# Gated linear attention inside a macaron decoder layer: the decay factors formed by running products on VectorE in place of TensorE sums, and small products grouped into fewer visits

## The reference

```python
h = h + 0.5 * swiglu(rmsnorm(h, ffn1_norm), ffn1_w_gu, ffn1_w_down)      # 1024 -> 2 x 2816 -> 1024
h = h + hybrid_mixer(rmsnorm(h, mix_norm), w_in, w_gk_up, b_gk, gla_out_norm, w_out, rel_bias)
h = h + 0.5 * swiglu(rmsnorm(h, ffn2_norm), ffn2_w_gu, ffn2_w_down)
h = h + sigmoid(rmsnorm(h, ple_norm) @ w_ple_gate) * (p @ w_ple_proj)
return rmsnorm(h, final_norm)

def hybrid_mixer(xn, ...):
    q_g, k_g, v_g, g_g, gk_lr, q_m, k_m, v_m = split(xn @ w_in)
    log_a = log_sigmoid(gk_lr @ w_gk_up + b_gk) / 16
    o_g = gla_chunked(q_g / 8, k_g, v_g, log_a)      # 4 heads, dk 64, dv 128:
                                                    # S_t = diag(exp(log_a_t)) S_{t-1} + k_t^T v_t ; o_t = q_t S_t
    o_g = rmsnorm(o_g, gla_out_norm) * silu(g_g)
    o_m = moba_attention(q_m, k_m, v_m, rel_bias)    # 8 heads of 64; at 256 tokens: causal softmax attention
    return concat(o_g, o_m) @ w_out                  # with a relative-position bias
```

## Time and profile before

| | us |
|---|---|
| median of 3 runs | 529.13 (528.93 to 530.37) |
| the profiled execution, its own time | 529.96 |
| its span | 528.0 |
| TensorE busy | 516.1 (98%) |
| VectorE busy | 329.3 (62%) |
| ScalarE busy | 274.7 (52%) |
| mean granted clock of TensorE | 0.995 |

### The profile page before, as it was taken

The page is one execution under the profiler, slowest core; times in us unless marked ns, Lnnn a source line. Parts: engine busy times, 40 slices in busy tenths (PEclk is TensorE's granted clock), DMA queues, the critical chain, the costliest instruction groups (busy, mean ns, idle before and its releaser), DMA issues.

```text
span 528.0 us, 7035 instructions
## 1 busy us (share of the span) xinstructions
PE 516.1 (98%) x2543; PEld 419.6 (79%) x2543; DVE 329.3 (62%) x436; ACT 274.7 (52%) x336; POOL 91.5 (17%) x169
## 2 busy tenths in 40 slices
PE   7999999999999999998999999999999999999994
PEld 4778888888788888876778888888888888888883
DVE  3687556565636374456997686565666556374675
ACT  4974454534435284875352865435444353452736
POOL 1504232223200110002221000222322232110000
PEclk9999999999999999999999999999999999999999
DMA  7999887786888766334459385888878867738202
GB/s 254 375 330 356 263 254 237 219 256 204 250 239 301 225 246 234 125 125 160 132 153 311 108 294 171 229 260 240 252 213 234 263 210 243 241 131 271 77 1 79
DMA packets 79464, 115.71 MB, mean 219 GB/s; under 512 B 5808, under 2 KB 51840, under 8 KB 79312
## 3 DMA queue, kind: packets, MB, share of 16 engines
q1 hardware_dynamic: 71472, 93.34, 57.0%
q0 software_dynamic: 7808, 21.99, 12.2%
q10 hardware_dynamic: 160, 0.07, 0.1%
HBM read 105.66 MB, written 11.28 MB: 221 GB/s over the span
## 4 chain that ended last, share of the span: by engine, by line
PE 92%; DVE 2%; SPq 2%; ACT 2%; DMA 1%; issue 1%; DVEq 0%; ACTq 0%
PE acc L561 86%; PE side L561 4%; SPq L439 1%; PE turn L601 1%; DMA raw<-in_ffn_w_gu 1%; PE turn L561 1%; ACT junk L932 1%; DVE w_lo L1209 0%; ACT w_hi L921 0%; DVE pr L1420 0%; SPq L429 0%; ACT L1179 0%; ACT L948 0%; DVE pr L1418 0%; DVE pr_sq L1439 0%
## 5 line engine op out<-in xcount | busy, mean ns | idle before, releaser
L1209 DVE TENSOR_TENSOR w_lo<-raw,w_hi 128x2048 fp32r<-128x2048 f32 (+1 forms) x87 | 192.6, 2216 | 104.8 <-ACT w_hi L921 104.7
L921 ACT ACTIVATE w_hi<-raw 128x2048 fp32r<-128x2048 f32 (+1 forms) x87 | 161.2, 1857 | 101.9 <-PE acc L561 99.9
L561 PE MATMUL acc<-w_hi,hT_hi 128*128 128x512 f32 x496 | 196.2, 396 | 0.2 <-DVE w_lo L1209 0.2
L561 PE MATMUL acc<-w_lo,hT_hi 128*128 128x512 f32 x496 | 193.5, 390 | 0.0
L561 PE MATMUL acc<-w_hi,hT_lo 128*128 128x512 f32 x496 | 193.4, 390 | 0.0
L561 PEld LDWEIGHTS acc<-w_hi,hT_hi 128*128 128x128 f32 x496 | 93.4, 188 | 22.2 <-issue 2.1
L561 PEld LDWEIGHTS acc<-w_hi,hT_lo 128*128 128x128 f32 x496 | 93.4, 188 | 19.8
L561 PEld LDWEIGHTS acc<-w_lo,hT_hi 128*128 128x128 f32 x496 | 93.5, 188 | 18.5
L487 POOL DMA_DIRECT2D act_in<-act_dram x92 | 50.1, 551 | 120.2 <-DMA act_dram<-act_sq 113.3
L561 PE MATMUL acc<-w_hi,a_hiT 128*128 128x512 f32 x176 | 68.6, 390 | 0.0
L561 PE MATMUL acc<-w_lo,a_hiT 128*128 128x512 f32 x176 | 68.5, 389 | 0.0
(11 more groups left out here) (170 smaller groups left out, 329.5 us busy)
## 6 DMA issues: line engine op xcount, KB each, us to landing
raw<-in_ffn_w_gu SPq DMA_DIRECT2D x82, 512.0 KB, 5.2
raw<-in_ffn_w_down SPq DMA_DIRECT2D x40, 512.0 KB, 5.3
raw<-in_w_in SPq DMA_DIRECT2D x24, 512.0 KB, 4.5
act_dram<-act_sq POOLq DMA_DIRECT2D x23, 256.0 KB, 5.5
act_in<-act_dram POOLq DMA_DIRECT2D x92, 64.0 KB, 3.6
raw<-in_w_out SPq DMA_DIRECT2D x8, 512.0 KB, 4.5
raw<-in_w_ple_gate SPq DMA_DIRECT2D x8, 512.0 KB, 5.5
raw<-in_ffn_w_gu SPq DMA_DIRECT2D x10, 256.0 KB, 6.2
```

The costliest lines, as they stand in the source:

```text
L561: return nc.tensor.matmul(o, lhsT, rhs, start=start, stop=stop, skip_group_check=True)
L921: A(w_hi[:, slot, :nk * N], raw[:, slot, :nk * N], ACT.Copy).then_inc(hi_ready, 1)
L1209: V.tensor_tensor(w_lo[:, slot, :nk * N], raw[:, slot, :nk * N], w_hi[:, slot, :nk * N].bitcast(F32), ALU.subtract).then_inc(lo_ready, 1)
```

## The change

**The decay factors.** `D0` to `D7`, `seg` and its load are gone. TensorE transposes `log_a` once (`T_a`, four transposes), ScalarE takes exp of it (`prefix`), and GpSimd fills `suffix` with ones. From level l-1 to level l, VectorE lengthens both running products in place (`widen`, two instructions of 128x256 per level; at level 7, 128x128), and then multiplies keys and queries in as before. Level 0 has no lower instruction: `lv0` takes `k_gT` itself. Level 7 is written to one row of `E` instead of two.

**The diagonal.** `diag` is gone. VectorE forms q times k and sums it per head (`dot`), and ScalarE writes eight 128x128 blocks `identity * qk` into `AT` (`dg`), which also replaces VectorE's clearing of `AT`.

**The transposes of q and k.** The block `qk_g` of `w_in` is now first. The gated q and k, and then the MoBA q, are turned through memory (`g_sq`, `q_sq` on VectorE, `nat_turn` on GpSimd's queue, `T_g0`, `T_g1`, `T_q` on ScalarE). The MoBA k stays with TensorE (`T_k0`, `T_k1`).

**The visits.** `z` uses all 128 rows (`gk_up` padded with zeros). The levels of both halves of the array are read out by one masked copy of 128x512 where there were two of 128x256. The scores moved from `side` to `turn`, `pv0` and `pv1` from `turn` to `side`. `lv1` stands right behind `T_k0`, `T_k1`; `lv3` behind `sc2`; `pv0` behind `sc3`; `pv2` behind `pvg1`.

**The softmax.** The division by the sums moved from VectorE to ScalarE (`nm0` to `nm3`, four instructions each, in place of VectorE's L1429 and L1430), and the buffer of the scores is doubled.

```diff
-WIN_BLOCKS = [("q_m", Q_M), ("k_m", K_M), ("qk_g", QK_G), ("v_m", V_M), ("v_g", V_G), ("g_g", G_G)]
+WIN_BLOCKS = [("qk_g", QK_G), ("q_m", Q_M), ("k_m", K_M), ("v_m", V_M), ("v_g", V_G), ("g_g", G_G)]
 MIX = {
+    (35, 0): ["lr"],                (35, 1): ["z"],              (37, 0): ["T_a"],
+    (38, 3): ["lv0"],               (40, 1): ["T_k0", "T_k1", "lv1"],
+    (40, 3): ["sc0.0", "sc0.1"],    (41, 0): ["lv2"],            (41, 2): ["sc1.0", "sc1.1"],
+    (42, 2): ["sc2.0", "sc2.1", "lv3"],                          (43, 2): ["sc3.0", "sc3.1", "pv0"],
+    (44, 3): ["pv1"],               (45, 1): ["pvg0"],           (45, 3): ["pvg1", "pv2"],
+    (46, 1): ["pv3"],               (47, 2): ["T_o0"],           (47, 3): ["T_o1"],
 }
-ACT_STEPS = [..., "hi38", "nat0", "hi39", "z", "hi40", "nat1", "T_k0", "D0", ...]
+ACT_STEPS = ["hi38", "tabE", "nat0", "z", "hi39", "T_a", "dg", "T_g0", "T_g1", "hi40", "nat1", "hi41", "hi42", "nat2", "T_q", "T_k0", "T_k1",
+             "hi43", "sc0", "nm0", "hi44", "sc1", "nm1", "nat3", "hi45", "sc2", "nm2", "hi46", "sc3", "nm3", "nat4", "pv0", "pv1", "hi47", "pvg", "pv2", "hi48", "pv3",
+             "nat5", "groot", "hi49"]
+DVE_STEPS = ["lr", "z", "g_sq", "zmin", "lo38", "la", "dot", "lo39", "Z0", "q_sq", "lv0", "lo40", "Z1", "Z2", "lo41", "lv1",
+             "sc0", "lv2", "lo42", "rc0", "Z3", "pr0", "sc1", "lo43", "rc1", "pr1", "sc2", "lv3", "lo44", "rc2", "pr2", "lo45", "sc3", "rc3", "pr3", "pv0", "lo46", "pv1", "lo47", "pvg", "pv2", "lo48", "pv3",
              "gg", "o_g", "lo49"]
...
+            def nat_turn(i):
+                pool.wait_ge(nat_turned, i + 1)
+                pool.dma_start(nat_dram[i], nat_sq[:]).then_inc(nat_out, 16)
+                pool.wait_ge(nat_out, 16 * (i + 1))
+                if i:
+                    pool.wait_ge(g_turned, 2)
+                for j in range(4):
+                    pool.dma_start(back[32 * j:32 * j + 32, :]..., nat_dram[i] in turned order).then_inc(nat_back, 16)
...
+            def widen(lv):
+                half, w = (1 << lv) // 2, 1 << lv
...
+                link(V.tensor_tensor(view(suffix[:], dims), view(suffix[:], dims), view(prefix[:], one, w - 1), ALU.mult))
+                dve.wait_ge(Z_ready, 2 * lv - 1)
+                return mark(V.tensor_tensor(view(prefix[:], dims, second), view(prefix[:], dims, second),
+                                            view(prefix[:], one, of_first), ALU.mult))
...
             def make_z(lv):
-                V.tensor_tensor(view(lower, dims), view(lower, dims), view(k_gT[:], dims), ALU.mult)
-                V.tensor_tensor(view(upper, dims, w), view(upper, dims, w), view(q_gT[:], dims, w), ALU.mult
+                if lv:
+                    V.tensor_tensor(view(z, dims), view(suffix[:], dims), view(k_gT[:], dims), ALU.mult).then_inc(Z_ready, 1)
+                    dve.wait_ge(dve_step, wide)
+                V.tensor_tensor(view(z, dims, w), view(prefix[:], dims, w), view(q_gT[:], dims, w), ALU.mult
                                 ).then_inc(Z_ready, 1)
```

More of the change, by code:

```diff
@@ L69 @@
 MIX = {
[L70 to L91, removed]
+    (35, 0): ["lr"],
+    (35, 1): ["z"],
+    (37, 0): ["T_a"],
+    (38, 3): ["lv0"],
+    (40, 1): ["T_k0", "T_k1", "lv1"],
+    (40, 3): ["sc0.0", "sc0.1"],
+    (41, 0): ["lv2"],
+    (41, 2): ["sc1.0", "sc1.1"],
+    (42, 2): ["sc2.0", "sc2.1", "lv3"],
+    (43, 2): ["sc3.0", "sc3.1", "pv0"],
+    (44, 3): ["pv1"],
     (45, 1): ["pvg0"],
-    (45, 2): ["pvg1"],
-    (46, 0): ["pv3"],
+    (45, 3): ["pvg1", "pv2"],
+    (46, 1): ["pv3"],
     (47, 2): ["T_o0"],
@@ L120, in chunks_of @@
     return 2 if U_PROJ <= u < U_GATE else CH
+PV_TURN = ("pv2", "pv3")
 def plan_turns():
@@ L136, in plan_turns @@
         for s in MIX[at]:
-            if s[:3] in ("T_q", "T_k", "T_g"):
+            if s in ("T_a", "T_k0", "T_k1"):
                 add(s, who="act")
-            elif s[:2] == "T_" or s[:2] == "pv" and s[:3] != "pvg":
+            elif s[:2] in ("T_", "sc") or s in PV_TURN:
                 add(s)
@@ L151, in plan_side @@
 def plan_side():
-    uses = [("gain0", "dve"), ("gain", "dve"), ("bias_row", "dve")]
+    uses = ["gain0", "gain", "bias_row"]
     for at in sorted(MIX):
         for s in MIX[at]:
[L157 to L168, removed]
+            if s[:2] == "lv":
+                uses += [f"{s}.{hh}" for hh in range(2)]
+            elif s[:2] not in ("T_", "sc") and s not in PV_TURN:
+                uses.append(s)
+    return {name: (i, i + 1) for i, name in enumerate(uses)}
 TURN, TURN_AT = plan_turns()
 SIDE = plan_side()
-SIDE_AT = {i: (who, c) for i, who, c in SIDE.values()}
 def turned(name, k=0):
@@ L228, in build @@
         grs = sb("grs", [P, M, GH])
+        qk = sb("qk", [P, M, GH])
         spare = sb("spare", [P, 4])
@@ L377, in build, with pv_bank @@
         block = ctx.enter_context(nc.Block())
+        def pv_bank(s):
+            return turn[:, TURN[s] % 2, :] if s in PV_TURN else side[:, SIDE[s][0] % 2, :]
         GU_W = [ffn1_w_gu, ffn2_w_gu]
@@ L546, in _ @@
             pool.dma_start(masks[:], pair_masks).then_inc(masks_in, 16)
+            pool.wait_ge(side_done, SIDE["z"][0] + 1)
+            nc.gpsimd.memset(suffix[:], 1.0).then_inc(ones_set, 1)
+            for i in range(2):
+                nat_turn(i)
             for pair in range(MH // 2):
@@ L1066, in step @@
[L1066 to L1073 removed]
+                    A(spare[:, 0:1], spare[:, 1:2], ACT.Exp)
+                elif s == "tabE":
+                    A(spare[:, 2:3], spare[:, 1:2], ACT.Exp)
+                elif s == "T_a":
+                    t = TURN[s]
+                    act_e.wait_ge(turn_done, t + 1)
+                    A(prefix[:], turn[:, t % 2, :], ACT.Exp).then_inc(turn_act, 1)
+                elif s == "dg":
+                    act_e.wait_ge(nat_turned, 1)
+                    act_e.wait_ge(dots, M)
+                    for m in range(M):
+                        for hd in range(GH):
+                            A(AT[:, 4 * (hd % 2) + 2 * (hd // 2) + m, :], ident[:], ACT.Copy, scale=qk[:, m, hd:hd + 1]
+                              ).then_inc(diag_set, 1)
```

355 lines of the change are left out of this document (196 added, 159 removed).

## The result

| | before | changed |
|---|---|---|
| median, us | 529.32 (4 runs, 528.93 to 530.37) | 523.50 (4 runs, 522.97 to 523.98) |
| ratio | | 0.9887 (95% interval 0.9872 to 0.9901) |
| profiled execution: own time, span | 529.96, 528.0 | 523.98, 522.1 |
| TensorE busy, us | 516.1 | 509.0 |

What follows compares the result with a forecast made beforehand. The prediction took TensorE's queue as the bound: 10.3 us leaves it, less waits of 1.4 at `pvg0` and 0.8 at the end, makes 8.1, so a median of 521.0. Its own range was 518.8 to 522.0, the wider one to 526.

Steps and rivals of the forecast that it cites:

- rivals 1 and 2: 1: the wait at `pvg0` also costs clock, 522.6, chance 0.26; 2: one turn is late, 524.9, chance 0.15.
- TensorE's queue, 10.3: Work leaving TensorE's queue: decay sums 3.6, transposes 1.4, `diag` with wait and slow clock 4.6, `z` 0.2, visits 0.5.
- rival 4: Merging visits saves nothing, as the 0.23 belongs to the small products: 521.5; counted within the forecast's 0.50.
- `T_a` and the first scores, no wait: TensorE would not wait: slack 0.6 at `T_a`; at `sc0` 2.8 for the keys, 7 for q.
- The first levels, no wait: Levels, turned through memory, ready at 219.1, asked for at 223.0: slack 3.9, no wait.
- Rival 3: Both turns through memory take what `h_turn` took: waits 8.2 and three clock drops, 531.8, slower; chance 0.05.
- `pvg0`, 1.4: TensorE waits 1.4 at `pvg0` for VectorE to read `pv0`'s bank; bounds 0 and 2.8.
- The end, 0.8: At the mixer's end `hT_lo` of `T_o0` is late by 0.8; bounds 0 and 1.4.
- five places: Possible TensorE waits: `T_a`, first levels and first scores at none, `pvg0` 1.4, the end 0.8.
- Rival 2: One turn late under a weight load: 2.3 wait at the first levels plus 1.6 of clock, 524.9; chance 0.15.
- The clock: Slow clock behind `diag`'s wait of 1.81: 1.0 in the 12 products and 0.6 in `diag`, 1.6 together.

Runs made afterwards that it cites:

- the split visits: visits_split: the changed kernel with `lv3` and `pv0` one chunk behind `sc2` and `sc3`, in visits of their own; 523.76 us.
- two_end_again: Second run of the changed kernel with two `w_out` loads held for the probabilities' turns and the gate's block taken ahead of `pv3`; 520.88 us.
- hold_three_end: Changed kernel, gate's block ahead of `pv3`, second to fourth `w_out` loads held until probability pairs 1, 3 and 4 are back; 522.31 us.
- hold_each_end: Changed kernel, gate's block ahead of `pv3`, second to fourth `w_out` loads held until probability pairs 2, 3 and 4 are back; 521.38 us.
- end_order: Changed kernel with `nat5` and `gg` ahead of `pv3`, last two weight units' splits behind the root and `o_g`, loads not held; 522.14 us.
- diag_later: The kernel before with `diag` one chunk later and `lv0` joined with `pv0` two chunks behind it; 529.03 us.
- hold_two: Changed kernel with the third and fourth `w_out` loads held on SyncE until the second and fourth pairs of probabilities are back; 520.76 us.

## Why the prediction was right and wrong

- **The number**: 521.0 was forecast, and 523.50 came out. That lies outside the forecast's own range, which ended at 522.0, and inside the range to 526 only because that took in rivals 1 and 2.
- **TensorE's queue, 10.3**: right, 10.3. The method (count by a row of the chain) held for every term, and rival 4, that joining visits saves nothing there, is refuted by 0.20 and 0.17 in the trace and by the split visits.
- **`T_a` and the first scores, no wait**: right. `T_a` started at 212.69 on the chain's clock, unhindered, and the MoBA q was copied at 234.8, 2.2 before its use.
- **The first levels, no wait**: right, but by less than I gave. I priced the four reads at 2.5; they took 4.8. GpSimd, ScalarE and VectorE of the changed kernel:

```profile
211.98 2.21 POOL L504 DMA_DIRECT2D back<-nat_dram  x4 [2.61 <-DMA nat_dram<-nat_sq]
```

```profile
218.53 0.63 ACT L1045 ACTIVATE q_gT<-back 128x512 f32<-128x512 f32 x1 [2.07 <-DMA back<-nat_dram]
```

```profile
219.81 0.43 DVE L1430 TENSOR_TENSOR E<-prefix,q_gT 128x256 f32<-128x256 f32 x1 [3.85 <-ACT k_gT L1045]
...
221.28 0.42 DVE L1430 TENSOR_TENSOR E<-prefix,q_gT 128x256 f32<-128x256 f32 x1
```

  The last factor is there at 221.7 instead of 219.1, and TensorE takes it up at 222.61: slack 0.9 instead of 3.9. The Trainium skill, "DMA: Bandwidth & Descriptors", section Anatomy of one DMA, gives 2.0 us plus bytes over 436 GB/s, an estimated 2.3 for such a read; no read of these turns did it (2.8 to 4.9). Rival 3 came closer than its 0.05 suggests, though its waits did not come about.
- **`pvg0`, 1.4**: the step was mis-sized and hidden. Where the turns don't hold TensorE up, VectorE's lateness is 0.8 (two_end_again, hold_three_end, hold_each_end); in the changed kernel it is 0.
- **The end, 0.8**: about 0.5 at `hT_lo`, and 0.35 more at the bank of `nat5`, which the forecast didn't have. In the profiles with end_order's edit and the loads held, `nat5` stands ahead of `pv3` and that short wait is not there.
- **What failed**: the list of "five places" where TensorE would wait. It left out `pv0`, `pv1` and `pv3`, so that their waits stood in the sum at nothing. I took the landing of the turns, 2.9 and 2.5, from medians over four pairs, of which only the last had met the weights in its write (4.71), and used them to price other transfers without asking what the change does to these. In it, the four pairs' writes are issued over 23.2 us (248.55 to 271.70) where it was 32.6 (239.03 to 271.63), TensorE asks for them with less to do in between, and the second to fourth load of `w_out` are issued about 4, 9 and 11 us earlier (at 252, 260 and 265 where it was 256, 269 and 276), because VectorE's splits, which free their slots, come earlier. The loads behind them, which met pair four's reads, start at 273.29 where it was 279.66. With 2.9 and 2.5 the second pair would have been there at 262.5 (254.92, 2.9, four issues 2.2, 2.5), 4.6 before `pv1`; it came at 268.70. The three waits together are 3.96 that the forecast lacks, less the 1.4 that it has at `pvg0` in its stead; the rest of the 2.5 is within the small terms.
- **Rival 2** (a turn late under a load of weights) had the mechanism right, with the wrong turn. Its price was too high by the drop of the clock, which the change's two profiles don't show.
- **The clock**: I had 1.6 for the drop behind a wait of 1.8. The price in TensorE's queue is about right: 2.82 less 1.36 for `diag`. In time it may be worth only half of that: the 35 runs of the kernel before give 0.8. What decides whether it comes is not settled. It came behind 1.81 and 1.84 at `diag` and 2.08 at `pv3`, and not behind 1.61, 1.89 and 1.60 in the change, nor behind 1.74 in diag_later.

With the turns on time the forecast would have been about right: hold_two runs at 520.76 where 521.0 was forecast. That closeness is in part luck: the waits left in it are other ones than the forecast's (0.39 at `pv0` and 0.29 at `pvg0`, where it had 1.4 at `pvg0` alone).

## What to carry to other kernels

When a change takes work from the engine that is the bound, everything that was slack against that engine becomes tight at once: list every instruction of the shortened stretch that waits for a transfer, the ones that the change does not touch first. Price a transfer by what else the DMA engines carry in the stretch where it will be, not by its median: the one slow instance of before (here 4.71 for the fourth pair) is the forecast for all of them. And a load that is needed only 19 or 24 us later (the third and fourth of `w_out`, issued at 259.96 and 264.82 and split from 279.07 and 288.91 on) can wait for a transfer that is needed now; two waits on the issuing queue brought 2.7 us, about half of the 5.8 that the rewrite had brought. A hold in a queue also holds all that stands behind it.

## What the runs showed of the hardware

- In the changed kernel the same write of 384 KB took 2.4 to 6.1 us of GpSimd's waiting, and the same read of 96 KB 2.3 to 7.2 us to land, the long ones where weight loads from another engine's queue were in flight. The Trainium skill, "DMA: Bandwidth & Descriptors", section Issuing engines are not separate DMA queues, says that all issuers end up on the same 16 engines and interleave; hold_two agrees, since waits in SyncE's queue alone brought the writes of pairs three and four back to 2.30.
- Idle times of TensorE of much the same length were followed by the 1.2 GHz level or not (1.81 was, 1.89 was not). The kernel before showed its drop at the same place in both of its profiles, and at least 10 of its 35 other runs had none. So a clock penalty is a term with a chance: the idle time alone doesn't decide it.
